# A hybrid decoder block: column sums and row scale by way of DRAM, first unit split by two engines, channel statistics as high and low parts

## What is computed

```python
h = rms_norm(x, g1)
z = h @ w_in                                   # 10 slices of 1024 columns
y_a = a_b * causal_conv3(a_c * a_h)
y_c = silu(layer_norm(causal_conv31(c_a * sigmoid(c_g)) + b))
v   = layer_norm(gelu(s_v))                    # over the 1024 channels
y_s = gelu(s_u) * (tril(ws[head]) @ v + bs)    # 8 heads, chunks of 128 tokens
m   = (sigmoid(g_a)*(y_a@wb0) + sigmoid(g_c)*(y_c@wb1) + sigmoid(g_s)*(y_s@wb2)) @ w_out
x   = x + rms_norm(m, g2)
x   = x + rms_norm(relu(rms_norm(x, g3) @ w_ff1)**2 @ w_ff2, g4)
```

## Time and profile before

| | |
|---|---|
| median of 3 runs | 961.3 us (961.15 to 962.46) |
| the profiled execution, its time | 959.98 us |
| the profiled execution, its span | 958.2 us |
| PE busy | 948.2 us (99%), 4838 instructions |
| VectorE busy | 731.4 us (76%) |
| ScalarE busy | 430.6 us (45%) |
| GpSimd busy | 104.4 us (11%) |
| HBM | 138.05 MB read, 4.19 MB written |

### The profile page before, as it was taken

One profiled execution on the slowest core, in us unless ns is written; L12 is line 12 of the kernel. 1 busy time (PEld: TensorE's weight loads), 2 busy tenths in 40 slices (PEclk: granted clock), 3 DMA queues, 4 the chain that ended last, 5 costly groups with the idle time before them and its releaser, 6 DMA issues.

```text
span 958.2 us, 13425 instructions
## 1 busy us (share of the span) xinstructions
PE 948.2 (99%) x4838; PEld 809.0 (84%) x4838; DVE 731.4 (76%) x854; ACT 430.6 (45%) x534; POOL 104.4 (11%) x128
## 2 busy tenths in 40 slices
PE   9999999999999999999999999999999999999997
PEld 7888888888888888888888888899889889979985
DVE  4679888888888988886584434599976886796698
ACT  7632333333333322224274323467745745754674
POOL 1100001001100011113100000131101102011110
PEclk9999999999999999999999999999999999999998
DMA  8333223322222122223225333477989679678864
GB/s 325 110 111 105 99 93 96 108 93 93 93 95 102 66 100 96 89 89 132 88 93 215 109 109 110 176 198 192 269 265 245 162 212 246 172 185 260 246 188 132
DMA packets 40731, 142.84 MB, mean 149 GB/s; under 512 B 4720, under 2 KB 4848, under 8 KB 40688
## 3 DMA queue, kind: packets, MB, share of 16 engines
q1 hardware_dynamic: 31728, 111.32, 32.7%
q0 software_dynamic: 7712, 27.27, 15.4%
q10 hardware_dynamic: 1248, 3.67, 1.1%
HBM read 138.05 MB, written 4.19 MB: 148 GB/s over the span
## 4 chain that ended last, share of the span: by engine, by line
PE 82%; DMA 7%; DVE 6%; ACT 3%; issue 2%; SPq 0%; POOL 0%; DVEq 0%; ACTq 0%
PE ps L1590 25%; PE ps L1592 24%; PE ps L1594 24%; DMA glu<-units_in 5%; DVE w_lo L1066 3%; PE ps L1775 2%; PE ps L1779 2%; PE ps L1777 2%; DMA raw_d<-units_in 1%; ACT w_hi L683 1%; PE ps L1716 1%; DVE h_lo L1066 1%; PE ps L1670 1%; ACT h L960 1%; DVE h L1408 1%
## 5 line engine op out<-in xcount | busy, mean ns | idle before, releaser
L1590 PE MATMUL ps<-a_hi,w_hi 128*128 128x512 f32 x576 | 225.7, 392 | 0.0
L1066 DVE TENSOR_TENSOR w_lo<-raw,w_hi 128x1024 fp32r<-128x1024 f32 (+1 forms) x125 | 153.3, 1229 | 94.1 <-ACT w_hi L683 93.4
L1592 PE MATMUL ps<-a_lo,w_hi 128*128 128x512 f32 x576 | 224.2, 389 | 0.0
L1594 PE MATMUL ps<-a_hi,w_lo 128*128 128x512 f32 x576 | 224.1, 389 | 0.0
L683 ACT ACTIVATE w_hi<-raw 128x1024 fp32r<-128x1024 f32 (+1 forms) x125 | 130.2, 1048 | 186.1 <-PE ps L1594 112.9
L1149 DVE SCALAR_TENSOR_TENSOR conf<-glu,cols,conf (+1 forms) x240 | 186.8, 778 | 27.5 <-DVE conf L1149 26.4
L1590 PEld LDWEIGHTS ps<-a_hi,w_hi 128*128 128x128 f32 x576 | 108.1, 188 | 22.7 <-issue 0.5
L1592 PEld LDWEIGHTS ps<-a_lo,w_hi 128*128 128x128 f32 x576 | 108.1, 188 | 22.6 <-issue 0.5
L1594 PEld LDWEIGHTS ps<-a_hi,w_lo 128*128 128x128 f32 x576 | 108.2, 188 | 22.5
L1066 DVE TENSOR_TENSOR w_lo<-glu,w_hi 128x1024 fp32r<-128x1024 f32 x56 | 67.7, 1221 | 37.0 <-ACT w_hi L683 36.9
L1590 PE MATMUL ps<-w_hi,h_hi 128*128 128x512 f32 x224 | 87.9, 393 | 0.4
(11 more groups left out here) (177 smaller groups left out, 1608.7 us busy)
## 6 DMA issues: line engine op xcount, KB each, us to landing
raw<-units_in SPq DMA_DIRECT2D x141, 512.0 KB, 3.2
glu<-units_in SPq DMA_DIRECT2D x26, 512.0 KB, 6.5
glu<-units_in POOLq DMA_DIRECT2D x26, 512.0 KB, 8.3
raw_d<-units_in POOLq DMA_DIRECT2D x24, 512.0 KB, 6.5
raw_v<-units_in SPq DMA_DIRECT2D x16, 512.0 KB, 5.9
raw_d<-units_in SPq DMA_DIRECT2D x8, 512.0 KB, 6.2
conf<-x_in SPq DMA_DIRECT2D x4, 512.0 KB, 6.0
conf<-x_in ACTq DMA_DIRECT2D x1, 2048.0 KB, 8.0
```

Source lines behind the costliest of these rows:

```text
L1066: return nc.vector.tensor_tensor(dst, src, hi, ALU.subtract)
L1590: nc.tensor.matmul(ps[:, bank, :], left_hi, right_hi, start=first, stop=False, skip_group_check=on_top)
L1592: nc.tensor.matmul(ps[:, bank, :], left_hi, right_lo, start=False, stop=False, skip_group_check=on_top)
L1594: return nc.tensor.matmul(ps[:, bank, :], left_lo, right_hi, start=False, stop=final, skip_group_check=on_top)
```

## The change

- The eight column sums are made once: SP loads all spatial weights in a second layout (512 KB, `wsr_in`, into the first part of `conf`), POOL masks them in one operation, VectorE reduces them (128 x 8 x 128 to 128 x 8) behind unit 4's work, ScalarE stores them to DRAM behind unit 5's, and POOL loads each head's row back, broadcast over the partitions. PE's product with ones goes.
- The row scale is stored to DRAM by POOL, element by element, and read back as a broadcast row into `row_rstd`. PE's `spread` and ScalarE's copy go. PE waits for `sumsq_ready` ahead of unit 4 and for `ident` ahead of the mixing stage.
- The normed tiles are made behind units 4 and 5 instead of 3 and 4.
- The first half of unit 0's `w_hi` is made by VectorE instead of ScalarE, and `gain` is loaded by POOL instead of ScalarE.
- The channel sum and the sum of squares are split into `stat_hi` (ScalarE) and `stat_lo` (VectorE), and each statistic is two fp32r products instead of one fp32 product.

The diff, with declarations of semaphores and tensors left out where a sentence above tells them:

```diff
-NORMED_BEHIND = {3: (0, 1, 2, 3), 4: (4, 5, 6, 7)}
+NORMED_BEHIND = {4: (0, 1, 2, 3), 5: (4, 5, 6, 7)}
...
+        stat_hi, stat_lo = over("stat_hi", [P, SEQ], "v_tile", dt=F32R), over("stat_lo", [P, SEQ], "room", dt=F32R)
+        sum_row = over("sum_row", [P, 2, P], "room")
+        ws_all = conf_flat[:, 0:D].rearrange("p (j t) -> p j t", j=KT)
...
@@ block.sync @@
             sp.dma_start(cols[:, :, :], cols_d).then_inc(cols_loaded, 16)
+            sp.wait_ge(sumsq_ready, 1)
+            sp.dma_start(ws_all, wsr_d).then_inc(ws_all_loaded, 16)
             with sp.Fori(3, U_FF // RAW) as i:
...
                         sp.wait_ge(s_step, 3 * KT)
+                        sp.wait_ge(stat_done, 2)
...
@@ block.gpsimd @@
             nc.gpsimd.memset(ones[:, :].bitcast(F32), 1.0).then_inc(consts_ready, 1)
+            pool.dma_start(gain[:, :], gain_d).then_inc(gain_loaded, 16)
             pool.wait_ge(consts_ready, 4)
...
             for c in range(CH):
                 inverse_rms(c, c)
+            pool.wait_ge(rstd_ready, CH)
+            pool.dma_start(rstd_d.rearrange("c p -> p c"), rstd[:, 0:CH],
+                           allow_slow_non_contiguous=True).then_inc(rstd_stored, 16)
...
+            def load_sums(j, slot):
+                pool.dma_start(sum_row[:, slot, :],
+                               col_sums_d[j:j + 1, :].to_broadcast([P, P])).then_inc(spatial_loaded[slot], 16)
...
             for j in range(2):
                 load_spatial(j, j)
+            pool.wait_ge(rstd_stored, 16)
+            pool.dma_start(row_rstd[:, :].rearrange("p (c t) -> p c t", c=CH),
+                           rstd_d.unsqueeze(0).to_broadcast([P, CH, P])).then_inc(row_rstd_ready, 16)
+
+            pool.wait_ge(ws_all_loaded, 16)
+            nc.gpsimd.affine_select(out=ws_all, in_=ws_all, compare_op=ALU.is_ge, fill=0.0, base=0,
+                                    pattern=[[0, KT], [-1, P]], channel_multiplier=1).then_inc(ws_all_masked, 1)
+            pool.wait_ge(sums_stored, 16)
+            for j in range(2):
+                load_sums(j, j)
 
             pool.wait_ge(bn_ready, 3 * CH)
...
                     load_spatial(j, j % 2)
-                mask_spatial(j % 2, 32 * (j // 2 + 1))
+                    load_sums(j, j % 2)
+                mask_spatial(j % 2, 48 * (j // 2 + 1))
...
@@ block.scalar @@
-            act.dma_start(gain[:, :], gain_d).then_inc(gain_loaded, 16)
...
-            act.wait_ge(half_loaded, 16)
-            copy_hi(w_hi[:, 0, 0:HALF], raw[:, 0, 0:HALF]).then_inc(half_hi, 1)
...
-                if n == CH - 2:
-                    act.wait_ge(rstd_spread, 1)
-                    nc.scalar.activation(row_rstd[:, :], ps[:, 2 * CH - 1, :], ACT.Copy).then_inc(row_rstd_ready, 1)
                 split_hi(u.plus(RING))
                 xn_hi(NORMED_BEHIND.get(n, ()))
+                if n == CH + 1:
+                    act.wait_ge(ws_summed, 1)
+                    act.dma_start(col_sums_d.rearrange("j s -> s j"), ws_sum[:, :],
+                                  allow_slow_non_contiguous=True).then_inc(sums_stored, 16)
...
+            act.wait_ge(ws_summed, 1)
             for b in range(2):
                 mix_tile(Count(U_MIX + PER_TILE * b), Count(b), b)
...
+                if j == 4:
+                    act.wait_ge(sq_sum, KT - 1)
+                    act.wait_ge(stat_done, 1)
+                    copy_hi(stat_hi[:, :], nrm[:, 0, :]).then_inc(stat_hi_ready, 1)
                 behind_branch(u)
+                if j == 0:
+                    act.wait_ge(chan_sum, KT)
+                    copy_hi(stat_hi[:, :], u_act[:, :]).then_inc(stat_hi_ready, 1)
...
@@ block.vector @@
+            dve.wait_ge(half_loaded, 16)
+            nc.vector.tensor_copy(w_hi[:, 0, 0:HALF], raw[:, 0, 0:HALF]).then_inc(half_hi, 1)
             dve.wait_ge(half_hi, 1)
...
-                    dve.wait_ge(row_rstd_ready, 1)
+                    dve.wait_ge(row_rstd_ready, 16)
...
                     lo(a_lo[:, k, :], xt[:, k, :], a_hi[:, k, :]).then_inc(act_lo_ready, 1)
+                if n == CH:
+                    dve.wait_ge(ws_all_masked, 1)
+                    nc.vector.tensor_reduce(out=ws_sum[:, :], in_=ws_all, axis=mybir.AxisListType.X,
+                                            op=ALU.add).then_inc(ws_summed, 1)
                 if n == CH + 1:
                     statistics(0)
...
-                nc.vector.scalar_tensor_tensor(out=bias[:, :], in0=ps[:, 7, 0:P],
+                nc.vector.scalar_tensor_tensor(out=bias[:, :], in0=sum_row[:, b, :],
...
+                if j == 4:
+                    dve.wait_ge(stat_hi_ready, 2)
+                    lo(stat_lo[:, :], nrm[:, 0, :], stat_hi[:, :]).then_inc(stat_lo_ready, 1)
                 add_branch(u, Count(KT + j), Count(j), j % 2)
                 split_lo(u.plus(1 + RING))
+                if j == 0:
+                    dve.wait_ge(stat_hi_ready, 1)
+                    lo(stat_lo[:, :], u_act[:, :], stat_hi[:, :]).then_inc(stat_lo_ready, 1)
...
@@ block.tensor @@
-            def spread():
-
-                pe.wait_ge(consts_ready, 5)
-                pe.wait_ge(rstd_ready, CH)
-                for c in range(CH):
-                    mm = nc.tensor.matmul(ps[:, 2 * CH - 1, c * P:(c + 1) * P], rstd[:, c:c + 1].to_broadcast([P, P]),
-                                          ident[:, :], start=True, stop=True)
-                mm.then_inc(rstd_spread, 1)
-
...
-                token_unit(Count(U_V + n), n, 0, c_hi, c_lo, {2: spread} if n == CH - 1 else {})
+                token_unit(Count(U_V + n), n, 0, c_hi, c_lo)
+            pe.wait_ge(sumsq_ready, CH)
             for n in range(CH, 2 * CH):
...
+            pe.wait_ge(consts_ready, 5)
             pe.wait_ge(act_lo_ready, KT)
...
-                    nc.tensor.matmul(ps[:, 7, 0:P], ones[:, :].bitcast(F32), ws_raw[:, b, :], start=True, stop=True)
...
-                if j == 1:
-                    pe.wait_ge(chan_sum, KT)
-                    nc.tensor.matmul(ps[:, 4, :], mean_of[:, :], u_act[:, :], start=True,
-                                     stop=True).then_inc(stat_done, 1)
-                if j == 4:
-                    pe.wait_ge(sq_sum, KT - 1)
-                    nc.tensor.matmul(ps[:, 5, :], mean_of[:, :], nrm[:, 0, :], start=True,
+                if j in (1, 4):
+                    n = (1, 4).index(j)
+                    pe.wait_ge(stat_lo_ready, n + 1)
+                    nc.tensor.matmul(ps[:, 4 + n, :], mean_of[:, :], stat_hi[:, :], start=True, stop=False)
+                    nc.tensor.matmul(ps[:, 4 + n, :], mean_of[:, :], stat_lo[:, :], start=False,
                                      stop=True).then_inc(stat_done, 1)
```

More of the change, by code:

```diff
@@ L235, in loads, with build @@
         return here if self.i is None else self.i * (16 * self.per // RAW) + here
-def build(nc, x_d, xt_d, gain_d, units_d, cols_d, rows_d, ws_d, bs_d, out_d):
+def build(nc, x_d, xt_d, gain_d, units_d, cols_d, rows_d, ws_d, bs_d, wsr_d, out_d):
     kept_d = nc.dram_tensor("mixed_kept", (SEQ, D), F32, kind="Internal").ap()
+    col_sums_d = nc.dram_tensor("spatial_sums", (KT, P), F32, kind="Internal").ap()
+    rstd_d = nc.dram_tensor("row_rstd", (CH, P), F32, kind="Internal").ap()
     with ExitStack() as ctx:
@@ L296, in build @@
         ident = sb("ident", [P, P])
-        mean_of = sb("mean_of", [P, P])
+        mean_of = sb("mean_of", [P, P], F32R)
         ones = sb("ones", [P, P], F32R)
@@ L360, in build @@
         gained_lo = sem("gained_lo")
-        rstd_spread = sem("rstd_spread")
+        rstd_stored = sem("rstd_stored")
         row_rstd_ready = sem("row_rstd_ready")
@@ L395, in build @@
         ws_masked = sem("ws_masked")
+        ws_all_loaded = sem("ws_all_loaded")
+        ws_all_masked = sem("ws_all_masked")
+        ws_summed = sem("ws_summed")
+        sums_stored = sem("sums_stored")
         spatial_done = sem("spatial_done")
@@ L407, in build @@
         stat_done = sem("stat_done")
+        stat_hi_ready = sem("stat_hi_ready")
+        stat_lo_ready = sem("stat_lo_ready")
         centred = sem("centred")
@@ L566, in _ @@
             nc.gpsimd.memset(ident[:, :], 0.0).then_inc(consts_ready, 1)
[L567 removed]
+            nc.gpsimd.memset(mean_of[:, :].bitcast(F32), 1.0 / D).then_inc(consts_ready, 1)
             nc.gpsimd.memset(ones[:, :].bitcast(F32), 1.0).then_inc(consts_ready, 1)
+            pool.dma_start(gain[:, :], gain_d).then_inc(gain_loaded, 16)
             pool.wait_ge(consts_ready, 4)
@@ L1618, in token_block, with token_unit @@
                 return mm
-            def token_unit(u, piece, half, hi, low, before_block={}):
+            def token_unit(u, piece, half, hi, low):
                 ready(u)
                 for c in range(CH):
-                    if c in before_block:
-                        before_block[c]()
                     mm = token_block(c, piece, hi, low, w_hi[:, u.ring, :], w_lo[:, u.ring, :],
@@ L1885 @@
```

(1 more changed line is left out.)

5 lines of the change are left out of this document (2 added, 3 removed).

## The result

The changed kernel takes 966.83 us (median of 6 runs, 965.37 to 969.86), the kernel before in the same comparison 961.06 (6 runs, 958.69 to 962.46). The ratio is 1.0067 with an interval of 1.0052 to 1.0082: slower, by 5.8 us between the medians, where 959.0 was forecast, within 957.3 to 961.0. The profiled execution took 966.97 us with a span of 965.2, 7.0 us more than the span before.

What follows compares the result with a forecast made beforehand. TensorE (PE) was taken to bound the kernel, with 82% of the span. The terms -0.92 - 1.76 - 0.25 + 0.5 + 0.58 - 0.42 sum to -2.27 us, from 961.3 to 959.0 us, with an 8-in-10 range of 957.3 to 961.0.

Steps and rivals of the forecast that it cites:

- slip of unit 7's landing: Weights of unit 7 land later beside the added DMA traffic; PE waits 0.5 us for it before unit 8.
- Spread of the row scale: Eight fp32 PE instructions that spread the row scale, starting at 26.05 us, go: 0.92 us gained.
- Column sums: Two fp32 PE instructions per tile go in the spatial products, over eight tiles: 1.76 us gained.
- First unit: Start of unit 0: gain on POOL's queue, w_hi half on VectorE; 0.25 us gained, range -0.4 to +0.6.
- Tie before unit 8: Before unit 8, a_lo is whole at 50.25 us and PE arrives at 50.29, so any slip becomes PE's wait.
- single floats crowd the weights: Rival, chance 0.25: row-scale store and broadcast hold unit 7's load by 2 us, PE waits before unit 8; 960.5 us.
- slower: Rival, chance 0.05: the row scale's DRAM round trip ends after 37.7 us, PE waits 6.5 us; 965.0 us.
- Round trip of the row scale: Before the mixing stage, store and broadcast back through DRAM end at about 35 us; VectorE needs the row at 37.7.
- signs that I had named for being wrong: Unit 7's landing late by 2 us or early, row scale after 37.7, or VectorE not following PE in the mixing stage.
- POOL's mask: POOL masks 1024 spatial-weight elements in 2.3 to 11.1 us, done between 33 and 42, needed at 42.8.
- First statistic: First channel statistic, near 430 us: PE waits for the split and weight reload, 1.0 us; a loss of 0.58 us.
- Second: Second channel statistic, near 464 us: two fp32r products replace fp32 ones without a PE wait; 0.42 us gained.

Runs made afterwards that it cites:

- e2: Changed kernel with the row scale stored as 128 runs of 16 bytes, in the wrong order, only timing counts: 959.05 us in a single run.
- e13: e12 with the row scale transposed by VectorE before its store and the column sums laid out in one piece per head: 956.92 us, ratio 0.9953.
- e4: Changed kernel with the row-scale part undone (spread on PE, normed tiles behind units 3 and 4): 960.97 us, ratio 0.9997 to the kernel before.
- e6: e4 with the gain loaded from ScalarE's queue as before, VectorE keeping the w_hi half: 958.84 us, ratio 0.9987 to the kernel before.
- e8: e2 plus a store of 512 single floats, each 512 bytes from the next, from the same queue: 962.86 us in a single run.
- e5: Changed kernel with twenty idle products of ones put in front of PE's wait for a_lo: 966.25 us.
- e12: e9 with the column sums transposed and stored as rows of 128 bytes: 962.28 us, ratio 1.0022 to the kernel before.
- e11: e6 with the column sums transposed by VectorE, stored as 128 rows of 128 bytes: 959.31 us, ratio 0.9984 to the kernel before.
- e3: Changed kernel with the column-sum part undone (no 512 KB load or reduction, PE's product with ones back): 971.35 us.
- e9: Changed kernel with row scale in 16-byte runs read with a stride, gain first on ScalarE's queue, reduction one unit later, first statistic one fp32 product: 962.86 us.

## Why the prediction was wrong

The forecast was 2.3 us faster, the measurement is 5.8 us slower. Two steps failed where it counts: the slip of unit 7's landing was put at 0.5 us and was 7.02, and the products at the lower clock behind the pause, 2.5 us, had no term. The steps in their order:

- *Spread of the row scale*, 0.92: right as a price. In e2, where PE doesn't wait before unit 8, unit 8 follows unit 1 by 38.08 us, before by 39.01. It is a gain only if nothing else becomes late; e13 has it.
- *Column sums*, 1.76: right, 8 x 0.21 = 1.7.
- *First unit*, -0.25 with bounds -0.4 lost to 0.6 gained: wrong, 2.16 lost. The step that failed is "POOL's queue is empty then, ScalarE's was not". The gain took 5.2 us there and 4.2 behind an x tile; the bound of 4.6 that I took from POOL's small loads (a median of two) lay too low, and I had no term for the clock, which fell to 0.50 behind the longer idle time: 1.18 us of the 2.16 are the late start, the rest is the pitch. e4 and e6 show it. In the changed kernel it cost nothing, since PE waited before unit 8 anyway.
- *Tie before unit 8*: the chain was right. 19.5 us from unit 7's copy to the whole `a_lo` were forecast and measured, the reduction was 1.22 (1.15 taken), and every microsecond of slip goes to PE.
- *Slip of unit 7's landing*, 0.5 with bounds 0 and 4.6: the step that failed, and nearly the whole miss. It was 7.02. I had sized it by a row of another kind, small loads of 64 KB in long runs, though no row showed a store of single elements, and I took the end of the range nearest to the existing contention. e2 and e8 show the mechanism: neighbouring single floats. The rival "single floats crowd the weights" had the place and the culprit right and charged 2 us. The rival "slower" came nearest in time (965.0, with a wait of 6.5 us), but by another path, the late return of the row scale; its number was luck.
- *Lower clock behind the pause*, missing: the second step that failed, 2.5 us (e5). No rival had it, not even the one with a wait of 6.5 us. The earlier trace rows had the price of such a stretch: 0.43 instead of 0.23 per product.
- *Round trip of the row scale*: I gave it until 37.7. The row was asked for at 34.60 and landed 5.6 us later, at 40.2, so it passed that mark, one of the signs that I had named for being wrong; but VectorE was itself late by 7 and wanted it at 44.7. The margin was gone for the same cause and didn't show.
- *POOL's mask*, 2.3 to 11.1: 1.11 us, below the range and without effect. *First statistic*: a loss of 0.58 forecast, 0.64 measured. *Second*: 0.42 gained, as forecast.

The 959.05 us of e2, where the store is mended and all else is the change, is nearly the forecast of 959.0. That is partly luck: it is one run, its first unit lost 2.2 us (unit 1 at 14.64) where 0.25 were to be gained, and that late arrival of PE hid that `a_lo` was whole only at 48.95 + 2.50 = 51.45, 1.2 us behind the 50.29 at which the forecast has PE there.

By the terms that held, e13, which has no such store and the old first statistic, should gain 0.92 + 1.76 + 0.42 = 3.1 us, and what its start brings (unit 1 at 12.11 in place of 12.45): 3.4. Its trace has 3.1 before the last 2000 products; the runs measured 4.5 (3.2 to 5.9, by the ratio).

Open: what the memory does with neighbouring single floats, and why the same store takes 9.0 us in one execution and 10.6 in another; why the feed-forward stage takes up to 4 us more in one profiled execution than in another; why e12's runs are slower than its trace explains; why e13 is 2.4 us below e11, where 1.3 were expected.

## What to carry to other kernels

Before a value from 128 partitions goes to DRAM, look at what one partition contributes to neighbouring addresses: with 4 bytes each, side by side, the store was slow here and so were the loads in flight, whichever queue it was on; turn it on chip first (0.2 us on VectorE), or give each partition at least 16 bytes in a row. When a prediction rests on a kind of transfer that no row shows, the range has to be open on that side, most of all where a tie leaves PE without slack. And charge a PE pause of several microseconds twice: for itself and for the products behind it at half pace.

## What the runs showed of the hardware

- Stores of single floats lying side by side: 0.5 KB in 7.9 us, 2 KB in 9.0 to 10.6, 4 KB in 9.3 to 10.8. The same 2 KB as runs of 16 bytes: 2.8 to 3.7 us. As single floats 512 bytes apart: 2.9 us. 16 KB as rows of 128 bytes: 1.4 to 4.2 us.
- 512 KB loads asked for within 2 us of such a store took 10.0 to 13.0 us, though they are on another queue; beside the quick stores they took 3.3 to 5.3. Those asked for later, while such a store was still in flight, took 7.1 us or more.
- Broadcasts of rows that lie in DRAM as four pieces of 128 bytes took 6.1 to 8.5 us when asked for at 51 to 57 us (e11, e12), and the weights asked for beside them 7.8 to 8.8; with the row in one piece of 512 bytes it was 4.4 at most and 5.0 (e13).
- PE's clock was at the 1.2 GHz level for about 5 us after a pause of 4.70 us (2.5 us lost) and for 6 us after one of 7.06 (e3), and stayed at 2.4 GHz after one of 0.80 behind filler products; behind pauses of 1.60, 1.7 and 2.5 us in e6, e12 and e9 the granted clock was 1.00 in the profiled executions. At the start of the changed kernel a pause of 1.95 us behind the warm-up was followed by a clock of 0.50 between 9 and 11 us.
- VectorE's multiplication of 128 x 512 fp32 with a gain and a row takes 0.66 us, and 1.05 when the row is read with a stride of four floats (four in a row: 2.74 and 4.29).
- A transposition of 128 x 32 fp32 on VectorE, in blocks of 32 x 32, takes 0.20 us. POOL masks 128 x 1024 elements in 1.11 us; for 128 x 128 it took up to 1.39.
- 4 KB for the gain, asked for at 1.3 to 1.4 us: 5.2 to 5.5 us from POOL's queue, 4.1 to 4.2 from ScalarE's behind an x tile, 2.8 ahead of it.
